# Eight modulation chunks first, sixteen between the pooling pieces, and nine gather buffers in the last stage

## What is computed

```python
mod = (jax.nn.silu(c) @ w_ada + b_ada)          # c: 1 + 8 rows, w_ada: 1024 x 6144
sh1, sc1, g1, sh2, sc2, g2 = jnp.split(mod, 6)
h = x * (1 + sc1) + sh1
q, k, v, u, gates = jnp.split(h @ w_in, ...)
pool_out, new_pool = pool_mixer(pool_buf, u, ...)  # windows 2, 4, 8, 16; then w_pool
attn_out = differential_attention(q, k, v, ...)
merged = g_pool * pool_out + g_attn * attn_out
x = layer_norm(alpha * x + (1 + g1) * (merged @ w_out))
h2 = x * (1 + sc2) + sh2
x = layer_norm(alpha * x + (1 + g2) * hier_moe(h2, ...))
```

## Time and profile before

| | us |
|---|---|
| median of 3 runs | 1842.24 (1841.55 to 1843.06) |
| the profiled execution | 1840.31 |
| its span in the trace | 1838.3 |
| stage 0 | 0 to 126.44 |
| stage 1 | 126.44 to 222.84 |
| stages 2 to 4 | 222.84 to 1746.7 |
| stage 5 | 1746.7 to 1838.3 |

### The profile page before, as it was taken

One profiled execution on the slowest core, in us unless ns is written; L12 is line 12 of the kernel. 1 busy time (PEld: TensorE's weight loads), 2 busy tenths in 40 slices (PEclk: granted clock), 3 DMA queues, 4 the chain that ended last, 5 costly groups with the idle time before them and its releaser, 6 DMA issues. The chain is left out here.

```text
span 1838.3 us, 25397 instructions
## 1 busy us (share of the span) xinstructions
PE 1463.8 (80%) x7980; PEld 1229.5 (67%) x7980; DVE 1024.6 (56%) x1528; ACT 855.6 (47%) x1401; POOL 268.9 (15%) x145
## 2 busy tenths in 40 slices
PE   7878696898888988889888897559946988999800
PEld 3347695787777877778777785447835777787600
DVE  1233424736457365473654737454655777898657
ACT  0022354555365553654546643321113777888611
POOL 0131111101011010110111100024431111111031
PEclk9989797998989999999999997778966999999955
DMA  9752221112031120311213111084315689666484
GB/s 332 238 165 67 81 58 58 47 54 73 26 104 46 47 76 26 103 46 35 84 30 100 49 46 46 15 284 138 104 38 184 236 289 322 221 210 206 148 240 129
DMA packets 202105, 220.54 MB, mean 120 GB/s; under 512 B 15055, under 2 KB 175963, under 8 KB 201916
## 3 DMA queue, kind: packets, MB, share of 16 engines
q1 hardware_dynamic: 168315, 152.23, 25.9%
q10 hardware_dynamic: 26760, 42.41, 6.3%
q0 software_dynamic: 6976, 25.23, 4.6%
HBM read 173.20 MB, written 46.86 MB: 120 GB/s over the span
## 5 line engine op out<-in xcount | busy, mean ns | idle before, releaser
L1154 ACT ACTIVATE R<-F 128x1024 fp32r<-128x1024 f32 (+3 forms) x310 | 302.3, 1016 | 241.1 <-DVE F L1571 106.9
L732 PE MATMUL S<-R 128*128 128x512 f32 (+1 forms) x528 | 216.0, 409 | 35.7 <-ACT R L1154 20.3
L2039 POOL TENSOR_TENSOR R<-F,R 128x1024 fp32r<-128x1024 f32 x40 | 98.0, 2451 | 832.3 <-ACT R L1154 832.3
L782 PE MATMUL PB<-R 128*128 128x344 f32 x616 | 212.0, 348 | 2.8 <-ACT F L1154 2.8
L733 PE MATMUL S<-R 128*128 128x512 f32 (+1 forms) x528 | 212.1, 402 | 0.0
L734 PE MATMUL S<-R 128*128 128x512 f32 (+1 forms) x528 | 211.6, 401 | 0.0
L783 PE MATMUL PB<-R 128*128 128x344 f32 x616 | 201.9, 331 | 0.0
L1154 ACT ACTIVATE F<-S,sm 128x256 f32<-128x256 f32 (+7 forms) x128 | 94.8, 741 | 160.3 <-DVE sm L1663 158.1
L782 PE MATMUL S<-R 128*128 128x344 f32 x440 | 147.1, 338 | 19.5 <-ACT R L1154 15.0
L732 PEld LDWEIGHTS S<-R 128*128 128x128 f32 (+1 forms) x528 | 101.4, 192 | 64.0 <-issue 37.4
L783 PE MATMUL S<-R 128*128 128x344 f32 x440 | 143.7, 330 | 0.0
(11 more groups left out here) (247 smaller groups left out, 2886.9 us busy)
## 6 DMA issues: line engine op xcount, KB each, us to landing
F<-in_w_ada SPq DMA_DIRECT2D x24, 1024.0 KB
F<-in_w_in SPq DMA_DIRECT2D x44, 512.0 KB, 4.0
F<-in_w_e_gate SPq DMA_DIRECT2D x16, 1024.0 KB, 7.0
F<-in_w_e_up SPq DMA_DIRECT2D x16, 1024.0 KB, 9.8
F<-in_w_e_down SPq DMA_DIRECT2D x16, 1024.0 KB, 8.2
y_d<-F ACTq DMA_DIRECT2D x32, 512.0 KB, 5.0
F<-in_x_prompt SPq DMA_DIRECT2D x16, 512.0 KB, 4.6
F<-in_cache_k SPq DMA_DIRECT2D x128, 64.0 KB, 1.9
```

Source lines behind the costliest of these rows:

```text
L732: mm(out, w[0], m[1], start=start, stop=False)
L782: mm(bank[:, 0:PIECE], whl[b][0][:, k, :], x[1][:, k, :], start=(k == 0), stop=False)
L1154: return nc.scalar.activation(out, in_, func, **kw)
L2039: nc.gpsimd.tensor_tensor(whl[c % 2][1], wraw2[c % 2], whl[c % 2][0].bitcast(F32), ALU.subtract).then_inc(w_lo.sem, 1)
```

## The change

It has three parts.

1. In stage 0 only eight chunks are computed (`EARLY`), those of shift1 and scale1, in the order 0, 4, 1, 5, 2, 6, 3, 7 (`CHUNK`). After two of them the columns of shift1 and scale1 for 256 features are there, and PE goes on with four of the sixteen parts of h (`x_columns`). x is loaded right after the first two chunks. The `+1` of the scale is done in the copy of the columns.
2. The other sixteen chunks are computed in stage 1 (`late`): two at its start, two after the pieces of each group, four before the last pooling and two after it. The rows of u are turned before these chunks (`turn_u`). Two buffers hold these chunks; their bank is `PB` or `Sb[3]`, and the pieces keep three banks. The rows are stored by SP's queue in place of ACT's, directly before the load that follows them.
3. In stage 5 each of the nine tiles has its own buffer `ya[t]`, and no gather waits for a store.

```diff
+    adaw = [f.take(KC * AW, KC, AW) for _ in range(2)]
+    ada_to = f.at
+    adaw.append(f.take(KC * AW, KC, AW))
+    EARLY = 8
+    CHUNK = [0, 4, 1, 5, 2, 6, 3, 7] + list(range(EARLY, NADA))
+    ABUF = [n % 3 for n in range(EARLY)] + [n % 2 for n in range(EARLY, NADA)]
...
-    ya = [f.take(D) for _ in range(6)]
+    ya = [f.take(D) for _ in range(NT + 1)]
...
# SP
+            def ada(n):
+                b, col = ABUF[n], CHUNK[n] * AW
+                if ada_turn(n) > 1:
+                    sp.wait_ge(ada_row, max(m for m in range(n) if ABUF[m] == b) + 1)
+                if n >= EARLY + 2:
+                    mod_store(n - 2)
+                sp.dma_start(adaw[b], w_ada[:, :, col:col + AW]).then_inc(ld_ada[b], 16)
+                sp.dma_start(badab[b][0:9, 0:AW], I["b_ada"][:, col:col + AW].to_broadcast([9, AW])).then_inc(ld_ada[b], 16)
+
+            ada(0)
+            ada(1)
+            for t in range(NT):
+                sp.dma_start(xr[:, t, :], x_p[t * P:(t + 1) * P, :]).then_inc(ld_x, 16)
+                if t == 3:
+                    ada(2)
+            sp.dma_start(xr[0:NS, NT, :], x_s).then_inc(ld_x, 16)
+            for n in range(3, EARLY):
+                ada(n)
...
+            ada(EARLY)
+            ada(EARLY + 1)
...
                 wchunk(UC + g * P, g % 2, None)
                 if g == 1:
                     sp.dma_start(wp32, I["w_pool"][0].rearrange("g p n -> p g n")).then_inc(wp_landed, 16)
+                if g >= 1:
+                    ada(EARLY + 2 * g)
+                    ada(EARLY + 2 * g + 1)
...
             chunk(0, 1)
+            for n in range(EARLY + 8, NADA):
+                ada(n)
# PE
+        for n in range(EARLY):
+            if n >= 4:
+                pe.wait_ge(ada_row, n - 3)
+            ada(n, Sb[n % 4])
+            if n >= 1:
+                modulation(n - 1)
+            if n >= 2 and n % 2 == 0:
+                x_columns(n // 2 - 1)
+        modulation(EARLY - 1)
+        x_columns(EARLY // 2 - 1)
...
+        def late(n):
+            if n >= EARLY + 2:
+                pe.wait_ge(ada_row, n - 1)
+            ada(n, (PB, Sb[3])[n % 2])
+
+        late(EARLY)
+        late(EARLY + 1)
         pe.wait_ge(ld_pool, 16)
...
+            if g:
+                turn_u(g - 1)
+            late(EARLY + 2 * g + 2)
+            late(EARLY + 2 * g + 3)
             if g:
                 pooling(g - 1)
+        turn_u(3)
+        for n in range(EARLY + 10, EARLY + 14):
+            late(n)
         pooling(3)
+        for n in range(EARLY + 14, NADA):
+            late(n)
         stage_end(pe, 1)
# DVE, group g of stage 1, between the window sums and the two splits
+            for n in {0: range(10, 14), 1: range(14, 16), 2: range(16, 18), 3: range(18, 22)}[g]:
+                late(n)
# POOL
-            if t >= 6:
-                out_st[t % 6].wait(pool, 16)
```

More of the change, by code:

```diff
@@ L262, in _build @@
     crow = f.take(D)
-    modrow = [crow[:, 256 * b:256 * b + 256] for b in range(3)]
-    badab = [f.take(256) for _ in range(3)]
+    AW = 256
+    modrow = [crow[:, D - AW * (b + 1):D - AW * b] for b in range(3)]
+    ada_from = f.at - 3 * AW
+    badab = [f.take(AW) for _ in range(3)]
     sTc = f.take(72, 8, 9)
-    AW = 256
-    adaw = [f.take(KC * AW, KC, AW) for _ in range(3)]
+    adaw = [f.take(KC * AW, KC, AW) for _ in range(2)]
+    ada_to = f.at
+    adaw.append(f.take(KC * AW, KC, AW))
     h32 = [f.take(512) for _ in range(2)]
@@ L272, in _build, with ada_turn @@
     NADA = NMOD * D // AW
+    EARLY = 8
+    CHUNK = [0, 4, 1, 5, 2, 6, 3, 7] + list(range(EARLY, NADA))
+    ABUF = [n % 3 for n in range(EARLY)] + [n % 2 for n in range(EARLY, NADA)]
+    def ada_turn(n):
+        return ABUF[:n + 1].count(ABUF[n])
+    ADA_TURNS = [ABUF.count(b) for b in range(3)]
     r = Pool_(R, NR)
@@ L304, in _build @@
     wp32 = f.take(1024, 4, 256)
+    uso = f.take(128)
+    assert f.at <= ada_from
+    f.at = ada_to
     upo = f.take(128)
-    uso = f.take(128)
     f_pool = f.at
@@ L563, in _ @@
             chunk(0, 1)
+            for n in range(EARLY + 8, NADA):
+                ada(n)
+            for n in range(NADA - 2, NADA):
+                sp.wait_ge(ada_row, n + 1)
+                mod_store(n)
+            for b in range(2):
+                sp.wait_ge(ada_st[b], 16 * ((NADA - EARLY) // 2))
             for b in range(2):
@@ L742, in _, with ada @@
         pe.wait_ge(cT_copied, 1)
+        def ada(n, bank):
+            pe.wait_ge(ld_ada[ABUF[n]], 32 * ada_turn(n))
+            for k in range(KC):
+                last = mm(bank[0:9, 0:AW], sTc[:, k, :], adaw[ABUF[n]][:, k, :], start=(k == 0), stop=(k == KC - 1))
+            last.then_inc(ada_done, 1)
         def modulation(n):
@@ L751, in modulation, with x_columns @@
             last.then_inc(modT_done, 1)
[L753 to L763, removed]
+        def x_columns(q):
+            for m in range(4 * q, 4 * q + 4):
                 if m == 0:
@@ L794, in _, with turn_u @@
         pe.wait_ge(stT_copied, 1)
-        def pooling(g):
+        def turn_u(g):
             piece_copied.wait_first(pe, 3 * g + 2)
@@ L1174, in _ @@
         act.wait_ge(h_hi, 17)
-        for b in range(3):
-            act.wait_ge(ada_st[b], 16 * NADA // 3)
         stage_end(act, 0)
@@ L1535, in _ @@
                 off_done.wait(act, u + 1)
-                act_(ya[u % 6][0:rows, :], ya[u % 6][0:rows, :], ACT.Identity, scale=rstd5[u % 3][0:rows, :], bias=off5[u % 3][0:rows, :]).then_inc(norm5.sem, 1)
+                act_(ya[u][0:rows, :], ya[u][0:rows, :], ACT.Identity, scale=rstd5[u % 3][0:rows, :], bias=off5[u % 3][0:rows, :]).then_inc(norm5.sem, 1)
     @block.vector
@@ L1609, in _, with late @@
         V(nc.vector.memset(sB[:, 0:16], 0.0))
+        def late(n):
+            ada_sum(n, (PB, Sb[3])[n % 2])
+        late(EARLY)
+        late(EARLY + 1)
         dve.wait_ge(stT_ready, 1)
@@ L1630, in _ @@
             mark(TT(plr[1], pooled, plr[0].bitcast(F32), ALU.subtract), pool_split, 2 * g + 2)
+        for n in range(22, NADA):
+            late(n)
         stage_end(dve, 1)
```

110 lines of the change are left out of this document (50 added, 60 removed).

## The result

The changed kernel took 1814.84 us (median of 4 runs, 1813.41 to 1819.87) where the kernel before took 1841.89 us (median of 4, 1840.57 to 1843.06). The ratio is 0.9858, with a 95% interval of 0.9837 to 0.988. A second measurement later, three more timed rounds and one profiled execution, gave 1812.1 us against 1841.28 us, 0.9828 [0.9789, 0.9868]. The forecast was 1817.1 us with a range of 1810 to 1828, and its sign and its size hold.

The account below looks back on a forecast made before the run. Loads were taken to bound stage 0 until about 46 us, PE after 62 us, and DVE stage 5. Terms of -59.6 + 46.7 - 12.2 = -25.1 us took 1842.2 to 1817.1 us, range 1810 to 1828.

Parts of the forecast that it names:

- Stage 0, -59.6 us: Stage 0, with eight chunks and x complete at 27.2 us, would go from 126.4 to 66.8 us.
- Stage 1, +46.7 us: Stage 1 would get 46.7 us longer, the sum of seven terms for late chunks, waits, poolings, a load and the tail.
- start of the first piece: Stage 1: after two chunks, the first piece would start 10.3 us in, before 6.1: +4.2 us.
- fourteen chunks: Stage 1: fourteen more chunks on PE at 3.55 us each, +49.7 us.
- poolings: Stage 1: shorter waits might leave PE's clock high, so each of four poolings gains 0.3 us, -1.2 us.
- chunk 20's load: Stage 1: it lands 7.1 us after chunk 18's last product, and chunk 19 covers 3.55 of that: +3.5 us.
- Stage 5, -12.2 us: Stage 5: without POOL's store waits, DVE's waits for gathers at tiles 4, 5 and 6 go, -12.2 us.
- The last stage gives less: Rival, stage 5: gathers meet outputs and x rows; 4 us won in place of 12 (1825), or nothing (1829); chance 0.09.
- The gaps cost clock: Rival, stages 0 and 1: five places with waits bring slow stretches and poolings gain nothing, +8 us: 1825; chance 0.14.
- Loads late in every pair: Rival, stage 1: 6 more waits of 3.5 us for loads at the chunk pairs, +21 us: 1838; chance 0.04.
- Slower, late chunks at the lower level: Rival, stage 1: late chunks at PE's lower level cost 3.3 us more each, 14 of them 46 us: 1863; chance 0.03.
- More is won: Rival, stage 1: no wait for chunk 20 (-3.5) and the full gain in the poolings (-4.8): 1809; chance 0.08.

Follow-up runs that it names:

- x1: The changed kernel with stage 5 put back as before: six gather buffers, and POOL waits for stores again; 1823.24 us, ratio 0.9903.
- x2: The kernel before with only the nine buffers of stage 5 changed; 1827.92 us, ratio 0.9926.
- x5: The changed kernel with chunks 14 and 17 moved behind the poolings of groups 0 and 1; 1811.02 us, ratio 0.9827.
- the three repairs: The edits of x3, x4 and x5, each made alone to the changed kernel and all together in x6; together 1798.36 us.
- x8: x6 with only chunk 8 at the end of stage 0 and chunk 9 at the start of stage 1; 1798.41 us, ratio 0.9769.
- x3: The changed kernel with DVE's splits ahead of the chunks' sums instead of behind them; 1808.17 us, ratio 0.9807.
- x6: The changed kernel with the edits of x3, x4 and x5 combined; 1798.36 us, ratio 0.9773.
- x4: The changed kernel with chunks 8 and 9 on PE at the end of stage 0; 1809.92 us, ratio 0.9821.
- x7: The changed kernel with late chunks behind the pooling, u turned directly before PE's wait, and DVE splitting first; 1836.0 us, ratio 0.9963.

## Why the prediction held, term by term

**Stage 0, -59.6 us, measured -59.5 us.** x was complete at 26.7 us (27.2 in the forecast). The wait that ended there, and the chunk after it:

```profile
26.71 1.09 PE L802 MATMUL T<-cst,F 128*128 128x128 f32 x8 [1.73 <-DMA F<-in_x_sample]
...
30.23 4.46 PE L782 MATMUL S<-F 128*9 128x256 f32 x16
```

That chunk took 0.8 us longer than the 3.62 us of the others. The last part of h was ready at 62.69 us, forecast 62.1, and the tail was 4.28 us where 4.65 was taken. The three profiles of the changed kernel ended the stage at 67.0, 66.0 and 65.4 us, so the path is as forecast, but the agreement to 0.1 us is luck.

**Stage 1, +46.7 us, measured +43.6 us.** This is the sum that was off most, by terms of both signs:

| term | forecast | measured | from |
|---|---|---|---|
| start of the first piece | +4.2 | +5.3 | 11.4 us into the stage, before 6.1 |
| first piece no longer slow | -1.4 | -1.4 | 0.42 us for its first product, before 0.62 |
| fourteen chunks | +49.7 | +49.4 | 3.46 us for seven of them, 3.55 to 3.62 for the others |
| waits for the splits | -7.8 | -8.3 | 9.1 us, before 17.4 |
| poolings | -1.2 | -2.6 | 18.9 us, before 21.5 |
| chunk 20's load | +3.5 | +2.8 | one wait of 2.82 us |
| tail | -0.3 | -1.5 | 1.9 us, before 3.3 |

The measured column adds up to +43.7, and +43.6 was measured. (The recorded terms of the start add up to 10.2 us and +4.1, not 10.3 and +4.2.) The mis-sized steps are these. The first chunk was taken as slow as the first piece of before, and took 6.37 us in place of 5.0. In the window of that chunk PEclk is 0.53, so nearly all of it ran at the lower level:

```profile
66.97:73.36 6.39, 6.37 (x16) 2.09 (x17) 0.29 (x4) 1.06 (x1) 0.30 (x1) 0.53 0.90 239
```

The fourteen chunks were sized right: one that stands ahead of another chunk takes 3.46 us (187.56 - 184.10), one ahead of a piece 3.55 us, and one ahead of a wait 3.62 us. The poolings gained more than twice of what was taken: 4.49, 5.19, 4.60 and 4.61 us, before 5.68, 5.08, 5.18 and 5.57 us. ACT's copies between the products do hold PE up, but only from about 4.5 us on, where 5.1 was assumed. PE's row for them in stage 1:

```profile
PE T L767 <- ACT F L1217: 2.2, 10, 0.3
```

The tail was 1.9 us (205.07 to 206.93) where 3.0 was taken. And chunk 20 was there 6.4 us after chunk 19 had begun (177.67 to 184.10 us), where 7.1 was worked out. The load was not faster than the 5.3 us of the estimate: from its issue at 178.68 us to PE's start at 184.10 us it is 5.4 us, with the bias and both of SP's issues in it. The step that failed is that these, 1.2 us in the forecast, were counted on top of the load and not inside its time; the row before it, with its store, took 1.0 us (177.67 to 178.68) in place of 0.6. The Trainium skill (DMA: Bandwidth & Descriptors, Anatomy of one DMA) gives a fixed cost of about 2.0 us and the bytes over 436 GB/s, fitted to transfers that GpSimd issues, and by that estimate the load takes 4.4 us and the wait would be 2.6 us. The measured waits (2.82, 2.86 and 2.79 us) are nearer to 2.6 than to my 3.5, but that doesn't confirm the 4.4 us: it lies 1.0 us under the 5.4 us of the rows, and the other terms were too large by about as much.

**Stage 5, -12.2 us, measured -12.4 us.** Three of DVE's four waits were indeed the price of three waits on POOL for outputs. DVE's wait at tile 2 stayed, 1.66 us. x1 and x2 confirm it from both sides (+11.8 and -12.2 us), so *The last stage gives less* falls. Nor were the DMA engines full there before, as that rival has it: their busy share was 0.77 from 1758 to 1781 us.

**Stages 2 to 4, 0, measured +4.2 us.** No term stood for them. Over all profiles the means of these stages differ by 1.0 us, so most of the 4.2 us belongs to the execution that was profiled; three more of the same kernel took 1813.41, 1813.46 and 1819.87 us. In the profile this +4.2 us nearly cancels the 3.1 us by which stage 1 was over-estimated, so that -24.1 us for a forecast of -25.1 us is in part luck. The medians fell by 27.1 and 29.2 us, 2 to 4 us more than forecast, on the side of stage 1's error.

**The rivals.** *The gaps cost clock* is true in part, and what I had named as a sign of being wrong (slow stretches follow the 2.4 us waits) did occur. In the changed kernel's first profile one of the four waits of 2.29 us was followed by one, the second:

```profile
143.42 0.43 PE L767 MATMUL T<-R 128*128 128x344 f32 x1 [2.29 <-DVE R L1702]
144.86 0.66 PE L767 MATMUL T<-R 128*128 128x344 f32 x1 [0.23 <-ACT F L1217]
```

```profile
144.80:148.00 3.20, 3.14 (x10) 2.67 (x11) 3.10 (x4) 1.55 (x5) 0.00 (x0) 0.50 0.70 247
```

In the window of 3.2 us PEclk is 0.50. But the stretch costs 0.6 us (5.19 for 4.60), not the 1.4 to 1.7 us that I took from the first piece. Only chunk 20 costs that much, 1.7 us in the second and third profile, so the five places together could cost about 4 us, not 8. *Loads late in every pair* falls: of the late chunks only chunk 20 waits. *Slower, late chunks at the lower level* falls: of sixteen late chunks one runs there in the first profile, chunk 8, which follows a wait of 6.34 us, and in the other two also chunk 20, in part. *More is won* is where the difference of stage 1 points, but only in small part for its reasons: the poolings gained 1.4 us more than forecast, not 4.8, and the wait for chunk 20 was there, 2.8 us, until x5 took it away.

## What to carry over

Independent work hides a wait only if it stands in the waiting engine's order between what feeds the wait and the wait itself. Moved past it, the same sixteen chunks and the same DVE work cost 23 us more, some 5.5 of them through a new queue on DVE. Where an engine serves two customers, one directly and one through a load that its result sets free, try both orders, and shorten the row of loads behind the loser at the same time: alone the three repairs gave 7, 4.5 and 3 us, and together 15. And before a difference of a few microseconds in an untouched stage is explained, profile both kernels again.

## What the runs showed of the hardware

PE's clock after a gap was not what I expected, a fixed answer to a given gap. The same wait, in the same place of the same kernel, was followed by the higher level once and by the lower level twice. Chunk 20 in the first, second and third profile of the changed kernel:

```profile
184.10 3.61 PE L782 MATMUL PB<-F 128*9 128x256 f32 x16 [2.82 <-DMA F<-in_b_ada]
```

```profile
182.84 5.30 PE L782 MATMUL PB<-F 128*9 128x256 f32 x16 [2.86 <-DMA F<-in_b_ada]
```

```profile
182.62 5.30 PE L782 MATMUL PB<-F 128*9 128x256 f32 x16 [2.79 <-DMA F<-in_b_ada]
```

The places of stage 1 in which PE waited (0.5 us or more) and then had a pooling or a late chunk to do, in the profiles of all kernels, with the poolings that had no wait for comparison. Chunk 9 of x8 is counted in.

| wait of PE | profiles | followed by the lower level |
|---|---|---|
| none (under 0.5 us), ahead of a pooling | x3, x6, x8 | 0 of 12 |
| 1.1 and 1.5 us, ahead of a chunk | x8, x6 | 0 of 2 |
| 2.29 us, ahead of a pooling | after three times, x1, x4, x5 | 11 of 24 |
| 2.7 to 2.9 us, ahead of a chunk | after three times, x1, x4, x7 twice, x8 | 5 of 8 |
| 4.1 to 4.9 us, ahead of a pooling or a chunk | before three times, x2, x3, x7 | 20 of 20 |
| 6.3 us and more | after three times, x1, x3, x5, x7 twice | 8 of 8 |

The lower level costs a pooling 0.5 to 1.5 us (4.5 to 4.6 us become 5.0 to 6.1), and a chunk 1.3 to 3.0 us. The Trainium skill (TensorE: Matmul & The Clock Gate, HAM oscillation) has it that waits between bursts bring PE back to the half clock again and again. The rows agree from 4.1 us on; between 2.3 and 2.9 us it happened in 16 of 32 cases, and one profile can't tell how the next will go. It is not an even chance at each place, though: after the wait of 2.29 us ahead of the first pooling it happened in 1 of 6 profiles, ahead of the second in 5, of the third in 3, of the fourth in 2. What decides it stays open. The twelve poolings without a wait never ran slow, which is a second gain of taking a short wait out.
